# Gates and B as one Strassen quad on the input sums of the C and H quad, values split around the queries, retention in the last value tiles

## The reference, cut to what matters

```
n = rms_norm(x, ln1_w)
q, k, v, g, gate_b, gate_c, hc = split(n @ w_in, 7 blocks of 512 columns)
o = retention_chunkwise(rope(q), rope(k) / sqrt(128), v, r0)      # 4 heads of 128, decay per head
o = group_norm_per_head(o) * ret_norm_w
ret_out = silu(g) * o
u = gate_c * hc
z = causal width-3 convolution of [conv_buf, u] over the tokens
conv_out = gate_b * z
x = x + concat(ret_out, conv_out) @ w_out
x = x + square(relu(rms_norm(x, ln2_w) @ w_up)) @ w_down          # 1024 -> 4096 -> 1024
```

## Time and profile before

| | |
|---|---|
| runs, median | 1352.94 us |
| the profiled execution | 1352.97 us, span 1351.2 us, granted TensorE clock 0.998 |
| PE busy | 1338.0 us (99% of the span) |
| PEld busy | 1205.0 us (89%) |
| DVE busy | 1010.3 us (75%) |
| ACT busy | 647.4 us (48%) |
| POOL busy | 177.7 us (13%) |
| DMA | 172.69 MB, mean 128 GB/s |

### The profile page before, as it was taken

One profiled execution on the slowest core, in us unless ns is written; L12 is line 12 of the kernel. 1 busy time (PEld: TensorE's weight loads), 2 busy tenths in 40 slices (PEclk: granted clock), 3 DMA queues, 4 the chain that ended last, 5 costly groups with the idle time before them and its releaser, 6 DMA issues.

```text
span 1351.2 us, 19022 instructions
## 1 busy us (share of the span) xinstructions
PE 1338.0 (99%) x7670; PEld 1205.0 (89%) x7670; DVE 1010.3 (75%) x1225; ACT 647.4 (48%) x763; POOL 177.7 (13%) x170
## 2 busy tenths in 40 slices
PE   8999999999999999999999999999999999999997
PEld 6888999899899899899888889998998998988986
DVE  6535978898967867868873569788988688587686
ACT  5311443468446446446534015435764454464564
POOL 2432200020000000000033241001100000000001
PEclk9999999999999999999999999999999999999999
DMA  8534361555545445455145343524664544635523
GB/s 284 168 98 157 71 187 33 135 130 143 139 115 139 141 107 154 125 125 156 32 137 167 94 133 76 175 64 125 124 174 125 125 126 125 149 101 136 145 63 109
DMA packets 106398, 172.69 MB, mean 128 GB/s; under 512 B 4228, under 2 KB 32004, under 8 KB 106312
## 3 DMA queue, kind: packets, MB, share of 16 engines
q1 hardware_dynamic: 82792, 127.11, 27.8%
q0 software_dynamic: 23232, 44.04, 19.3%
q10 hardware_dynamic: 288, 0.33, 0.1%
HBM read 164.06 MB, written 7.41 MB: 127 GB/s over the span
## 4 chain that ended last, share of the span: by engine, by line
PE 98%; DMA 0%; ACT 0%; issue 0%; POOL 0%; DVE 0%; SPq 0%; DVEq 0%; POOLq 0%; ACTq 0%
PE pair L932 37%; PE pair L1012 28%; PE pair L759 16%; PE pair L1025 8%; PE pair L767 4%; PE pair L810 2%; PE pair L829 1%; PE pair L833 1%; PE pair L838 1%; DMA w_raw<-in_w_in 0%; PE pair L841 0%; PE pair L851 0%; PE pair L862 0%; POOL rstd L1632 0%; PE pair L845 0%
## 5 line engine op out<-in xcount | busy, mean ns | idle before, releaser
L1275 ACT ACTIVATE ring<-raws 128x1024 fp32r<-128x1024 f32 x272 | 285.0, 1057 | 304.5 <-PE pair L1012 150.2
L1998 DVE TENSOR_TENSOR ring<-raws,ring 128x1024 fp32r<-128x1024 f32 x272 | 328.7, 1219 | 98.7 <-ACT ring L1275 97.3
L932 PE MATMUL pair<-mlp_in_hi,ring 128*128 128x320 f32 x1792 | 396.5, 309 | 0.0
L1012 PE MATMUL pair<-ring,a_ring 128*128 128x512 f32 x1632 | 380.4, 390 | 0.0
L1012 PEld LDWEIGHTS pair<-ring,a_ring 128*128 128x128 f32 x1632 | 305.5, 188 | 63.6
L932 PEld LDWEIGHTS pair<-mlp_in_hi,ring 128*128 128x128 f32 x1792 | 300.1, 188 | 0.7
L932 PE MATMUL pair<-mlp_in_lo,ring 128*128 128x320 f32 x896 | 276.7, 309 | 0.0
L932 PEld LDWEIGHTS pair<-mlp_in_lo,ring 128*128 128x128 f32 x896 | 168.1, 188 | 0.2
L1948 DVE TENSOR_TENSOR x<-x,pair 128x512 f32<-128x512 f32 x160 | 103.4, 679 | 11.7 <-PE pair L1012 11.7
L759 PE MATMUL pair<-pair_a,norm_hi 128*128 128x512 f32 x320 | 100.6, 395 | 0.5 <-ACT norm_hi L1180 0.5
L759 PE MATMUL pair<-ring,norm_hi 128*128 128x512 f32 x320 | 100.4, 395 | 0.0
(11 more groups left out here) (195 smaller groups left out, 1740.4 us busy)
## 6 DMA issues: line engine op xcount, KB each, us to landing
raws<-in_w_mlp_up SPq DMA_DIRECT2D x32, 1024.0 KB, 5.7
raws<-in_w_mlp_down SPq DMA_DIRECT2D x32, 1024.0 KB, 5.2
w_raw<-in_w_in SPq DMA_DIRECT2D x19, 1024.0 KB, 5.1
raws<-in_w_mlp_up POOLq DMA_DIRECT2D x16, 1024.0 KB, 9.6
raws<-in_w_mlp_down POOLq DMA_DIRECT2D x16, 1024.0 KB, 8.7
past_state<-in_state_ret SPq DMA_DIRECT2D x16, 512.0 KB, 4.8
raws<-in_w_in SPq DMA_DIRECT2D x8, 1024.0 KB, 9.0
raws<-in_w_out SPq DMA_DIRECT2D x8, 1024.0 KB, 5.4
```

The source lines that it names most:

```text
L932: mm = pe.matmul(out[:, n, 0:HALF], item_half(item, h, a)[:, k, n * P:(n + 1) * P], tokens[c][:, k], start=(i in (B11, B21, SUM_1112, B22) ...
L1012: mm = pe.matmul(out[:], a_item[:, a, 2 * h + k, pair * P:(pair + 1) * P], item_half(item, h, c)[:, k], start=(i in (B11, B21, SUM_1112) a ...
L1275: nc.scalar.activation(item_half(item, h, 0), raw_half(quad, RAW_OF[i], h), ACT.Copy).then_inc(half_hi.sem, 1)
L1998: nc.vector.tensor_tensor(item_half(item, h, 1), raw_half(quad, RAW_OF[i], h), f(item_half(item, h, 0)), ALU.subtract).then_inc(half_lo.se ...
```

## The change

- **G and B** leave the groups of tokens and features. A second quad of the up kind holds them, first B and then G: quad 1 with blocks (CONV_B, GATE_G) of w_in. It has the same seven inputs as the quad of C and H, and PE runs `up(CH)`, then `up(OUT)`, then `down(OUT)`. The quads are 11 in place of 10 and the items 77 in place of 70.
- **Order of the groups**: K 0 to 4, V 0 and 1, Q 0 to 4, V 2 to 4. The retention of the prompt stands behind V 2, V 3 and V 4. Its last two steps and all turns of "o" stand inside the first halves of `up(CH)`. "so" is one step for four heads, and the four past states have buffers of their own.
- **The low parts** of items B11, B21 and B22 of quads 0 and 1 are made on POOL (`plain_low`), 12 halves a layer. SUM_1112 of quads 0, 1 and 3 is summed by DMA (before: only that of the first up quad of the MLP).
- **B22's product** is accumulated in the bank of SUM_1112's (start is dropped), so `hidden_mix` goes in all quads.
- **The gate** is applied in feature order: after the quad's sums ACT makes sigmoid(-g) of a half (`gate_of`), DVE multiplies (`finish_gate`, `gate_out`). The convolution runs on DVE during the first products of `up(OUT)`. It is multiplied by B in three steps (`first_conv_done`, `second_conv_done`).

The core of the diff:

```diff
-W_IN_ORDER = [1, 2, 0, 3, 4]
-GATE_C, CONV_IN = 5, 6
-GROUPS = ([("K", p) for p in range(NT)] + [("V", p) for p in range(NT)] + [("Q", p) for p in range(NT)]
-          + [("G", t) for t in range(NT)]
-          + [("B", ft, h) for ft in range(FT) for h in range(2)])
+W_IN_ORDER = [1, 2, 0]
+GATE_C, CONV_IN, CONV_B, GATE_G = 5, 6, 4, 3
+GROUPS = ([("K", p) for p in range(NT)] + [("V", p) for p in range(2)] + [("Q", p) for p in range(NT)]
+          + [("V", p) for p in range(2, NT)])
-GAPS = {("V", 2): [("s", 0)],
-        ("Q", 0): [("s", 1)],
+GAPS = {("Q", 0): [("s", 0)],
+        ("Q", 1): [("s", 1)],
         ("Q", 2): [("S", 0)],
         ("Q", 3): [("S", 1)],
-        ("Q", 4): [("Y", 1), ("R", 1), ("S", 2), ("so", 0)],
-        ("G", 0): [("Y", 2), ("R", 2), ("S", 3)],
-        ("G", 1): [("Y", 3), ("R", 3), ("S", 4), ("so", 1)],
-        ("G", 2): [("Y", 4), ("R", 4)]}
+        ("Q", 4): [("so", 0)],
+        ("V", 2): [("Y", 1), ("R", 1), ("S", 2)],
+        ("V", 3): [("Y", 2), ("R", 2), ("S", 3)],
+        ("V", 4): [("Y", 3), ("R", 3), ("S", 4)]}
+LAST_SMALLS = [("Y", 4), ("R", 4)]
-BY_DMA = (2, SUM_1112)
+BY_DMA = [0, 1, 3]
+PLAIN = [(item, h) for item, h in ITEM_HALVES if item // PRODUCTS < 2 and item % PRODUCTS in (B11, B21, B22)]
...
# PE, turn()
+                elif what == ("o", ORDER[3]):
+                    pe.wait_ge(hidden_summed.sem, hidden_summed.at(layer, c_sums_to(CH, B21, 0)))
...
                 elif kind == "o":
-                    pe.wait_ge(o_gated.sem, o_gated.at(layer, what[1] + 1))
+                    pe.wait_ge(o_scaled.sem, o_scaled.at(layer, STAT[ORDER.index(what[1])] + 1))
...
# PE, up_half()
-                                               start=(i in (B11, B21, SUM_1112, B22) and (k, m) == (0, 0)),
+                                               start=(i in (B11, B21, SUM_1112) and (k, m) == (0, 0)),
...
# PE, up()
+                            if (b, i, h) == (CH, B11, 1):
+                                for s in LAST_SMALLS:
+                                    small(layer, s)
+                                for p in (0, 1):
+                                    turn(layer, ("o", ORDER[p]))
+                                up_half(b, i, h, lambda: turn(layer, ("o", ORDER[2])))
+                            elif (b, i, h) == (CH, B21, 1):
+                                up_half(b, i, h, lambda: [turn(layer, ("o", ORDER[p])) for p in (3, 4)])
+                            elif (b, i, h) == (CH, SUM_ALL, 0):
+                                up_half(b, i, h, lambda: turn(layer, ("past",)))
...
+                up(CH)
                 up(OUT)
-                wait_unit(layer, 4, 0)
-                for n in range(3):
-                    free_bank(n)
-                    b_product(n, range(HALF_K))
...
# ACT, behind the groups
+                copy_v(4)
+                weight_half(1, 0)
+                ch_hi_of(0)
+                weight_half(1, 1)
+                read_turn(layer, ("o", ORDER[0]))
+                read_turn(layer, ("o", ORDER[1]))
+                copy_product(CH, B11, 0)
+                read_turn(layer, ("o", ORDER[2]))
+                weight_half(2, 0)
...
+                weight_half(8, 0)
+                first_tap(0)
+                first_tap(1)
+                weight_half(8, 1)
+                first_tap(2)
+                first_tap(3)
+                weight_half(9, 0)
+                copy_product(OUT, B11, 0)
+                weight_half(9, 1)
...
+                weight_half(13, 0)
+                gate_of(1, 0)
+                weight_half(13, 1)
+                gate_of(1, 1)
+                weight_half(14, 0)
+                gate_of(0, 0)
+                weight_half(14, 1)
+                gate_of(0, 1)
...
# POOL
+                def plain_low(item, h):
+                    quad, i = divmod(item, PRODUCTS)
+                    pool.wait_ge(half_hi.sem, half_hi.at(layer, 2 * item + h + 1))
+                    settle(pool)
+                    nc.gpsimd.tensor_tensor(item_half(item, h, 1), raw_half(quad, RAW_OF[i], h),
+                                            item_half(item, h, 0).bitcast(f32), ALU.subtract).then_inc(plain_lo.sem, 1)
...
+                plain_low(B21, 0)
+                group_norm(layer, 3)
+                finish_o(layer, 3)
+                plain_low(B21, 1)
+                group_norm(layer, 4)
+                finish_o(layer, 4)
+                add_last_to_12(0)
+                add_third_to_11(0)
+                plain_low(B22, 0)
+                plain_low(B22, 1)
+                plain_low(PRODUCTS + B11, 0)
+                add_half(1, 0)
+                plain_low(PRODUCTS + B11, 1)
+                add_half(1, 1)
+                plain_low(PRODUCTS + B21, 0)
+                plain_low(PRODUCTS + B21, 1)
...
# DVE, behind Q 4
+                stats(layer, 0)
+                ch_made(0)
+                norm_heads(layer, 0)
+                ch_made(1)
+                read_small(layer, ("Y", 1))
...
+                read_small(layer, ("Y", 3))
                 stats(layer, 3)
+                read_small(layer, ("R", 3))
+                read_small(layer, ("S", 4))
                 norm_heads(layer, 3)
+                ch_made(3)
+                read_small(layer, ("Y", 4))
                 stats(layer, 4)
+                read_small(layer, ("R", 4))
+                ch_made(4)
                 norm_heads(layer, 4)
                 ch_made(5)
                 ch_lo_of(0)
+                hidden_sum(CH, B21, 0)
                 weight_half(2, 0)
...
# DVE, from the end of up(CH): second_u(0), second_u(1), two small copies into tail, then
+                conv(0)
+                conv(1)
+                weight_half(9, 0)
+                conv(2)
+                conv(3)
+                weight_half(9, 1)
+                weight_sum(1, SUM_111222, 0)
+                weight_sum(1, SUM_111222, 1)
+                hidden_sum(OUT, B21, 0)
...
+                hidden_sum(OUT, SUM_1222, 1)
+                finish_gate(1, 0)
+                weight_half(13, 1)
+                finish_gate(1, 1)
+                gate_out(1)
+                hidden_sum(OUT, B22, 0)
+                weight_half(14, 0)
+                weight_sum(2, SUM_1112, 0)
+                hidden_sum(OUT, B22, 1)
+                finish_gate(0, 0)
+                weight_half(14, 1)
+                finish_gate(0, 1)
+                gate_out(0)
+                weight_sum(2, SUM_1112, 1)
...
+                a_item_lo(OUT, B11)
+                second_conv_done(0)
+                a_item_lo(OUT, B21)
+                weight_half(15, 0)
+                second_conv_done(1)
                 sample_lo(OUT, 1)
                 sample_lo(OUT, 0)
                 down(OUT)
```

More of the change, by code:

```diff
@@ L145, with is_down, up_quad @@
 SUMS = [(SUM_1112, 0), (SUM_1112, 1), (SUM_111222, 0), (SUM_111222, 1)]
-BY_DMA = (2, SUM_1112)
+BY_DMA = [0, 1, 3]
 def sums_to(quad, product, half):
-    assert (quad, product) != BY_DMA
-    skipped = 2 if (quad, product) > BY_DMA else 0
+    assert product != SUM_1112 or quad not in BY_DMA
+    skipped = 2 * sum((q, SUM_1112) < (quad, product) for q in BY_DMA)
     return quad * len(SUMS) + SUMS.index((product, half)) + 1 - skipped
+def is_down(quad):
+    return quad >= 2 and quad % 2 == 0
+def up_quad(b):
+    return 2 * b + 3 if b >= 0 else b + 2
 def up_item(b, i):
-    return (2 * b + 2) * PRODUCTS + i
+    return up_quad(b) * PRODUCTS + i
 def down_item(b, i):
-    return (2 * b + 3) * PRODUCTS + i
+    return (2 * b + 4) * PRODUCTS + i
 def mlp_steps():
-    out = []
+    out = [("up", CH, i, h) for i in range(PRODUCTS) for h in range(2)]
     for b in range(OUT, NBLK):
@@ L708, in _ @@
                 settle(sp)
[L709 to L710 removed]
+                for h in range(H):
+                    sp.wait_ge(state_out[h].sem, state_out[h].at(layer, 16))
                     settle(sp)
@@ L777, in turn @@
                 last = n - 2 if kind != "n2" else n - 4 if what[1] in (2, 4) else -1
+                if kind == "tail":
+                    pe.wait_ge(hidden_summed.sem, hidden_summed.at(layer, c_sums_to(OUT, B22, 0)))
+                    last = TURN["past",]
+                elif what == ("o", ORDER[3]):
+                    pe.wait_ge(hidden_summed.sem, hidden_summed.at(layer, c_sums_to(CH, B21, 0)))
+                elif kind == "past":
+                    pe.wait_ge(hidden_summed.sem, hidden_summed.at(layer, c_sums_to(CH, B22, 0)))
+                elif kind == "n2" and what[1] == 1:
+                    last = TURN["tail",]
                 if last >= 0:
@@ L814, in small @@
                 n = SMALL[what]
-                out = small_bank[n % 3]
-                kind, p = what
-                needs = [n] if kind == "s" else [max(n - 2, SMALL["s", 1] + 1)]
+                banks = [bank[i] for i in SMALL_BANKS[what]]
+                out, (kind, p) = banks[0], what
+                needs = [banks_read(what)]
```

(27 more changed lines are left out.)

659 lines of the change are left out of this document (296 added, 363 removed).

## The result

The changed kernel takes 1362.18 us (1362.03 to 1362.64), beside 1352.97 for the kernel before on the same chip. The ratio is 1.0068, 95% interval 1.0056 to 1.0081: slower by 9.2 us. The forecast was 1351.9 us with a range of 1343 to 1357. The profiled execution has a span of 1360.3 us and a mean granted clock of 0.995 (before: 1351.2 and 0.998).

A forecast was written before the change was run, and what follows sets the result against it. PE was taken to bound the kernel: 1352.97 us less 12.1 of PE's work, plus 11.0 of stalls (0.9 + 3.1 + 1.5 = 5.5 a layer), gives 1351.9 us. The range was 1343 to 1357.

The forecast's parts named there:

- a: In up(CH), at the turn of o's fourth tile: PE waits for DVE's hidden_sum(CH, B21, 0), 0.9 us a layer.
- c: At the start of down(OUT): PE waits 0.9 us for the first input and 0.6 for sample rows, 1.5 a layer.
- PE's work: G and B's old products go, the new quad comes: net 6.05 us a layer less, 12.1 over two.
- one product in eight of G and B: Remark on PE's net saving of 6.05 us a layer, as a share of what G and B cost.
- POOL's low half: A low half made on POOL takes 2.4 us, against 1.22 on DVE.
- rival of longer halves: At a and c's neighbour in up(OUT), POOL's halves exceed 2.4 us: 4 us more per us; chance 0.16, slower.
- The lock, with POOL in front: In up(OUT), POOL's low half (8, 1) starts first and holds DVE's convolution up by 2.25 us.
- the rival in which it costs nothing: In up(OUT) at SUM_1112, POOL is the one that waits, not DVE: 1347.4 us; chance 0.20.
- The rival without waits: PE doesn't wait at all, DVE being further ahead: 1340.9 us, up to 1344; chance 0.14.
- The rival of an overlooked wait: PE held at some item by 2 us or more a layer: 1356 and above; chance 0.02 slower, 0.06 same.
- stall b: In up(OUT), at SUM_1112: PE waits for hidden_sum(OUT, B21, 0), 0.9 us from DVE's queue plus 2.25 hold-up, 3.1 a layer.

The follow-up runs named there:

- e7: Changed kernel with DVE reordered before the first gate product and around the layer outputs, and ACT at the layer's start: 1341.6 us, ratio 0.9916.
- e3: Changed kernel with item 8's two low halves made on DVE instead of POOL: 1352.93 us.
- e10: Changed kernel with the first adding transfer, add_half(1, 0), cut to half its rows (result not the reference's): 1357.41 us.
- e1: Changed kernel with DVE's order in up(OUT) altered, putting B21's sums ahead of the last two convolution tiles: 1347.01 us, ratio 0.9956.
- e2: Changed kernel with the two copies into tail moved behind the second B21 sum: 1362.14 us.
- filler runs: Changed kernel with small identity products on PE before the first gate product: 1366.35 us with 44, 1358.17 us with 22.
- e8b: Changed kernel with item 8's two low halves put in front of the transfer add_half(1, 1) in POOL's order: 1359.73 us.
- e4b: Changed kernel with 22 small float32 identity products on PE in front of the first gate product: 1358.17 us.
- e9: Changed kernel with all twelve plain low halves made on DVE, none on POOL: 1351.29 us.

## Why the prediction was wrong

**What held.** The three places of the waits. a: 1.0 us a layer (forecast 0.9). c: 1.9 (1.5, within 0 to 2.5), though otherwise divided: 1.7 at the first input where 0.9 was forecast, 0.2 at the sample where it was 0.6. PE's work: e7 has only 1.4 us of new waits and is 11.3 faster, so the 12.1 stand (12.7 by this run). The remark that this is one product in eight of G and B doesn't come out, 6.05 of 55.45 us being one part in nine; no sum used it. POOL's low half: 2.41 us alone in the rows above (2.4), so the rival of longer halves is out, and the kernel is slower by another way. The lock, with POOL in front: the rival in which it costs nothing is refuted by e3 against the changed kernel. The rival without waits is what e7 comes near to, but only by another order. The rival of an overlooked wait is out too: no other new wait is in the rows.

**The step that failed: the sum for stall b.** It had 0.9 for DVE's queue and 2.25 for one low half, 3.1 us a layer; the wait is 5.5. The mechanism was right and its size was not. Two things in it:
- The 0.9 fits (e3, by subtraction). The hold-up was 4.6, since not one but both low halves of item 8 lay in front of the taps. I walked DVE's, ACT's and PE's queues but gave POOL's transfers no time. And POOL's queue holds `add_half(1, 0)` and `add_half(1, 1)` in this very stretch. The second stands idle for 2.4 us until the first has landed, and both low halves come behind it. With that idle time gone (e10) the wait was 3.4. A row of the kernel before showed the same effect, in its MLP, and I didn't read it (POOL in order of time; the transfer before it on this queue starts at 286.94):

```profile
293.46 1.29 POOL L1716 DMA_DIRECT2D raws<-in_w_mlp_up  x1 [5.20 <-issue]
```

- The edges of the lock were too narrow. I named the taps, with their two SBUF inputs, as what is held. The copy with one input was held just so (4.79 us for 0.17), in the changed kernel and in e1. The Trainium skill (SBUF — State Buffer, section "SBUF: two separate sides") counts an operation of VectorE in a two-port performance mode among those that take the pair, beside those with two SBUF inputs. That would cover the copy; that it ran in such a mode is no row's to say. It moved nothing in the sum, since the tap behind it would have been held instead (e2). What isn't held shows in e10, where POOL's two low halves run from 172.47 to 177.76 us. The DVE operations with one input in PSUM (`pair`) take the same 0.69 and 0.28 us as elsewhere; the copies after them are held:

```profile
174.02 0.69 DVE L2126 TENSOR_TENSOR u<-pair,hidden 128x512 f32<-128x512 f32 x1 [1.98 <-PE pair L950]
174.62 0.28 DVE L2127 TENSOR_TENSOR u<-pair,hidden 128x128 f32<-128x128 f32 x1
174.94 0.50 DVE L2231 COPY tail<-u 128x8 f32<-128x8 f32 x1
175.35 2.48 DVE L2233 COPY tail<-u 128x64 f32<-128x64 f32 x1
```

**The term that was missing: the clock.** I priced a wait at its length. Behind b the granted clock was 0.50, and the slow start costs 3.9 us in all. With b's own error of 4.7 us over both layers (10.9 for 6.2), c's of 0.8 and a's of 0.3, that is 9.7 of the 10.3 us between forecast and result. The Trainium skill (TensorE: Matmul & The Clock Gate, section "Part 1: The HAM clock gate") says that the clock has these two levels and follows how busy TensorE has been recently. The filler runs agree: same wait, busy engine, clock 1.00.

## What to carry to other kernels

When work moves to an engine with its own queue, walk that queue with its transfers in it: one that has to wait for an earlier one holds everything behind it. Price a long wait of TensorE above its length: here waits of 2.1 to 5.5 us cost 0.3 to 3.0 us more behind them, and one of 1.7 us brought no slow clock. Then look for the operation that TensorE needs soonest and put it ahead of filler work on DVE: here three reorderings turned +9.2 us into -11.3. An operation held by a lock costs only when somebody waits for what is queued behind it.

## What the runs showed of the chip

- **The clock after a wait varies.** The surplus behind wait b was 1.6 and 2.3 us after 5.5 and 5.4 us of waiting, 2.6 and 1.8 after 4.1 and some 4.0 (e8b), 3.0 and 0.3 after 3.4 on the mean of the two (e10), 1.8 and 0.3 after 2.1 twice (e3). The 0.3 are there at a clock of 1.00 as well (e4b), so in these layers the clock didn't fall. Behind the 1.7 us of wait c it stayed at 1.00 (232 to 240 us of the changed kernel). The length of the wait alone doesn't set it. It differs between executions too: the ten of e3 took 1351.45 to 1353.61 us, the shorter ones at a mean clock of 0.999 and the longer ones at 0.997 or 0.998.
- **POOL didn't get in between DVE operations on SBUF that follow each other.** A multiplication of 128x512 that takes 1.29 us by itself took 3.85 at 132.26 in the changed kernel (`finish_o`). DVE ran two operations on two SBUF inputs from 132.10 to 134.98 meanwhile; POOL ended at 136.11, 1.2 us after DVE had begun one with an input in PSUM (134.90, `c<-c,pair`). In the other direction a DVE operation waits through two POOL operations in a row.
- **A transfer on POOL's queue behind one of 512 KB started 0.2 to 0.4 us after that had landed**, 6.0 to 8.8 us after its start, whether POOL works in between or not (in e9 it stood idle for 4.80 us). Behind one of 256 KB it didn't have to wait for the landing (e10).
- **A float32 product of 128x128 on the identity shows as two records**, 9.82 us for 44 of them, 0.22 each.
